# One program instead of two, four heads turned earlier, both mLSTM gates from one weight tile, and one activation table set asked for in two layer norms

## What is computed

```python
def third_block(x, ...):
    x = layer_norm(x, in_ln_g, in_ln_b)
    proj = x @ w_in[l]
    q, k, v, o_pre, i_pre, f_pre, z, xbc, dt_raw, g_a, g_b = jnp.split(proj, splits, -1)
    h_a = mlstm_branch(q, k, v, o_pre, i_pre, f_pre, ...)   # 8 heads; i_pre, f_pre: 8 columns each
    h_b = mamba2_branch(z, xbc, dt_raw, ...)
    merged = jax.nn.sigmoid(g_a) * (h_a @ p_a[l]) + jax.nn.sigmoid(g_b) * (h_b @ p_b[l])
    x = layer_norm(ALPHA * x + merged @ w_out[l], ln1_g[l], ln1_b[l])
    u = causal_dwconv(x @ w_up[l], f_conv_w[l], f_conv_b[l])
    u_gate, u_val = jnp.split(u, 2, -1)
    return layer_norm(ALPHA * x + (jax.nn.silu(u_gate) * u_val) @ w_down[l], ln2_g[l], ln2_b[l])
```

## Time and profile before

| | |
|---|---|
| median of 3 runs | 2726.02 us (2725.89 to 2728.17) |
| profiled execution, its own time | 2728.42 us |
| its span, first to last instruction | 2726.6 us |
| PE busy | 2544.7 us, 93% |
| PEld busy | 2024.6 us, 74% |
| DVE busy | 1384.9 us, 51% |
| ACT busy | 650.0 us, 24% |
| POOL busy | 1537.7 us, 56% |
| mean granted clock of PE | 0.965 |

### The profile page before, as it was taken

How to read it: one execution, slowest core, us unless ns; L and a number is a source line. 1 busy time by engine, 2 the same in 40 slices (tenths; PEclk the granted TensorE clock), 3 DMA queues, 4 the chain that set the end, 5 groups by cost and what they waited for, 6 DMA issues and landing times. The chain is left out here.

```text
span 2726.6 us, 32321 instructions
## 1 busy us (share of the span) xinstructions
PE 2544.7 (93%) x11714; PEld 2024.6 (74%) x11714; DVE 1384.9 (51%) x1929; ACT 650.0 (24%) x1047; POOL 1537.7 (56%) x1039
## 2 busy tenths in 40 slices
PE   6998999999989997799999998899998998999997
PEld 4885678888777773588967876766887886878775
DVE  6886651221489997668024335133356144535354
ACT  2116620110353344330022123123113222200002
POOL 2640266766688884468625745424762665566551
PEclk8999999999999998899999999899999999999998
DMA  8640023233222221122221322211331222223221
GB/s 268 218 158 1 31 78 93 93 94 107 93 78 78 77 92 46 50 93 93 77 77 47 108 63 66 68 53 47 108 93 32 77 79 91 77 93 93 93 71 42
DMA packets 231014, 231.36 MB, mean 85 GB/s; under 512 B 10011, under 2 KB 228860, under 8 KB 230780
## 3 DMA queue, kind: packets, MB, share of 16 engines
q1 hardware_dynamic: 228368, 228.87, 26.4%
q10 hardware_dynamic: 2540, 1.11, 0.2%
HBM read 227.86 MB, written 2.10 MB: 84 GB/s over the span
## 5 line engine op out<-in xcount | busy, mean ns | idle before, releaser
L1264 POOL TENSOR_TENSOR Wl<-raw,Wh 128x512 fp32r<-128x512 f32 (+4 forms) x772 | 1048.3, 1389 | 29.1 <-issue 7.6
L1258 POOL TENSOR_SCALAR Wh<-raw 128x2048 fp32r<-128x2048 f32 (+3 forms) x197 | 369.5, 1876 | 953.1 <-PE PS L1311 541.4
L1311 PE MATMUL PS<-Hh,Wh 128*128 128x512 f32 x1984 | 790.3, 398 | 76.4 <-POOL Wl L1264 24.8
L1311 PE MATMUL PS<-Hl,Wh 128*128 128x512 f32 x1984 | 783.3, 395 | 0.0
L1311 PE MATMUL PS<-Hh,Wl 128*128 128x512 f32 x1984 | 782.2, 394 | 0.0
L1311 PEld LDWEIGHTS PS<-Hh,Wh 128*128 128x128 f32 x1984 | 376.3, 190 | 176.5 <-issue 48.1
L1311 PEld LDWEIGHTS PS<-Hh,Wl 128*128 128x128 f32 x1984 | 376.3, 190 | 83.9 <-issue 1.5
L1311 PEld LDWEIGHTS PS<-Hl,Wh 128*128 128x128 f32 x1984 | 376.7, 190 | 80.0 <-issue 0.7
L1311 PE MATMUL PS<-Bh,Wh 128*128 128x512 f32 x688 | 271.5, 395 | 8.8 <-DVE Bl L2841 8.8
L1311 PE MATMUL PS<-Bl,Wh 128*128 128x512 f32 x688 | 270.0, 393 | 0.0
L1311 PE MATMUL PS<-Bh,Wl 128*128 128x512 f32 x688 | 269.8, 392 | 0.0
(11 more groups left out here) (442 smaller groups left out, 2885.1 us busy)
## 6 DMA issues: line engine op xcount, KB each, us to landing
raw<-in_w_in SPq DMA_DIRECT2D x44, 1024.0 KB, 5.8
raw<-in_w_ff SPq DMA_DIRECT2D x32, 1024.0 KB, 5.3
raw<-in_conv_w_in SPq DMA_DIRECT2D x24, 1024.0 KB, 5.1
raw<-in_ret_w_in SPq DMA_DIRECT2D x24, 1024.0 KB, 5.2
spare<-in_ada_w SPq DMA_DIRECT2D x20, 1024.0 KB, 7.2
raw<-in_w_up SPq DMA_DIRECT2D x20, 1024.0 KB, 5.4
raw<-in_w_out SPq DMA_DIRECT2D x8, 1024.0 KB, 5.0
raw<-in_conv_w_out SPq DMA_DIRECT2D x8, 1024.0 KB, 5.0
```

The lines of the kernel that those rows point to most:

```text
L1258: pool.tensor_scalar(st.Wh[0:rows, slot, k, 0:g.width], st.raw_slot(slot)[0:rows, k, 0:g.width], 1.0, 1.0, ALU.mult, ALU.mult)
L1264: ins = pool.tensor_tensor(st.Wl[0:rows, slot, k, 0:g.width], st.raw_slot(slot)[0:rows, k, 0:g.width], st.Wh[0:rows, slot, k, 0:g.width].b ...
L1311: mm = pe.matmul(out, lhs, rhs, start=(k == parts[0][0] and n == 0), stop=(k == parts[-1][0] and n == 2))
```

## The change

All of it is done at once:

- **One program.** Stages w1 and w2 become one: one list of steps, one weights_part with one set of semaphores (weights_sems). The semaphores that zeroing clears are given back there, so that later parts can have them.
- **One tile for both gates.** i_rows and f_rows become gate_rows, 40 columns wide: two loads (pieces) put the input gate's 8 columns at column 0 and the forget gate's at column 32 of the same slot; the columns between hold what was there and are multiplied too. ACT copies partitions 0 to 7 and 32 to 39 of the result to their two places (two_gates). All later tiles move to the other slot.
- **Four heads turned early.** The turns of heads 0 and 1 (PE) go between two pieces of ga in head 7, ahead of the values of head 6, those of heads 2 and 3 ahead of head 7's last scores; the first waits for all 32 exponentials. On ACT the four outs go around the squares of head 6, ahead of ga's last take.
- **One table set.** A CentredNorm without pre (l1 and l2) asks for the set that has both Exp and Ln at its start.

```diff
...
 M_HEADS, M_CONV = 8, 4
+GATE_ROWS = 32
 S_HEADS, S_GROUPS, S_CONV = 16, 4, 4
...
         CURRENT.remove(s)
+    for step in steps:
+        if isinstance(step, Part):
+            step.ctx.close()
     return part
...
         act.drain()
+        if not self.pre:
+            act.preload_act_table_set(EXP_AND_LOG)
         for c in range(KC if self.pre else 0):
...
-    def __init__(self, w, rhs, rounds, phases, stride=2 * TW, mode="features", row0=0, rows=D, width=TW, ready=None):
+    def __init__(self, w, rhs, rounds, phases, stride=2 * TW, mode="features", row0=0, rows=D, width=TW, ready=None, pieces=None):
         self.w, self.rhs, self.rounds, self.phases, self.mode = w, rhs, rounds, phases, mode
         self.row0, self.rows, self.stride, self.width, self.ready = row0, rows, stride, width, ready
-        self.k_order = None
+        self.k_order, self.pieces = None, pieces
         self.made_by = self.beside = self.beside_load = self.after = self.early = None
...
+
+    def loads(self):
+
+        return len(self.pieces) if self.pieces else 1 + (self.rows % P > 0)
...
-def weights_part(nc, st, name, steps):
+def weights_sems(nc, name):
     ctx = ExitStack()
-    landed = sems(nc, ctx, name, "landed0 landed1")
-    freed = sems(nc, ctx, name, "acc_free0 acc_free1")
-    split_done, multiplied, staged, posted, taken, asked, made, rounded = sems(
-        nc, ctx, name, "split_done multiplied staged posted taken asked made rounded")
+    return ctx, sems(nc, ctx, name, "landed0 landed1 acc_free0 acc_free1 split_done multiplied staged posted "
+                                    "taken asked made rounded")
+
+
+def weights_part(st, ctx, weight_sems, steps):
+
+    landed, freed = weight_sems[0:2], weight_sems[2:4]
+    split_done, multiplied, staged, posted, taken, asked, made, rounded = weight_sems[4:]
     base = stage0 = post = made0 = 0
...
         for j in range(g.rounds * len(g.phases)):
-            landings[(base + j) % 2] += 1 + (g.rows % P > 0)
+            landings[(base + j) % 2] += g.loads()
         base += g.rounds * len(g.phases)
...
-        per = 1 + (g.rows % P > 0)
+        per = g.loads()
         before = sum((g.base + q) % 2 == slot for q in range(p))
...
                 dst = st.raw_slot(slot)
+                if g.pieces:
+                    for at, c0, n in g.pieces:
+                        sp.dma_start(dst[:, 0:full, at:at + n], body[:, :, ds(c0, n)]).then_inc(landed[slot], 16)
+                    continue
                 sp.dma_start(dst[:, 0:full, 0:g.width], body[:, :, ds(c0, g.width)]).then_inc(landed[slot], 16)
...
             pe.wait_ge(scaled, h + 1)
+            if h == 0:
+                pe.wait_ge(exped, NB * M_HEADS)
             if h >= 2:
...
             beside.products(pe, j, (k0 + h % 2,))
+            if h == M_HEADS - 1:
+                turn(0)
+                turn(1)
             if h:
...
             beside.products(pe, j, (k0 + 3,))
+            if h == M_HEADS - 1:
+                turn(2)
+                turn(3)
             score(h, 3)
         values(M_HEADS - 1)
-        for h in range(GROUP):
-            turn(h)
         rows_beside.products(pe, 0, range(KC))
...
                 beside.take(act, h // 2 - 1)
+            if h == M_HEADS - 1:
+                out(0)
+                out(1)
             if h:
                 squares(h - 1)
+        out(2)
+        out(3)
         beside.take(act, M_HEADS // 2 - 1)
...
         rstd(1)
-        for h in range(GROUP):
-            out(h)
         rows_beside.take(act, 0)
...
-def program(nc, t, out, stop=None):
+def program(nc, t, out):
     ctx = ExitStack()
...
-        def rows_to(c, n):
-            def act(e, acc, i, p):
-                return e.activation(st.A[0:n, c, :], acc[0:n, 0, :], ACT.Copy)
-            return act
+        def two_gates(e, acc, i, p):
+            e.activation(st.A[0:M_HEADS, 24, :], acc[0:M_HEADS, 0, :], ACT.Copy)
+            return e.activation(st.A[0:M_HEADS, 25, :], acc[GATE_ROWS:GATE_ROWS + M_HEADS, 0, :], ACT.Copy)
...
                                   pre=(pcols("final_norm_2", 8), 1e-6))
-            i_rows, f_rows = (
-                tiles(w3, H, 1, at_i + n * M_HEADS, width=M_HEADS, act=rows_to(24 + n, M_HEADS), order="gate",
-                      ready=norm7_8.ready) for n in range(2))
-            gates, gates_rest = gates_parts(nc, st, f_rows.all_staged)
+            gate_rows = tiles(w3, H, 1, at_i, width=GATE_ROWS + M_HEADS, act=two_gates, order="gate",
+                              ready=norm7_8.ready, pieces=[(GATE_ROWS * n, at_i + n * M_HEADS, M_HEADS) for n in range(2)])
+            gates, gates_rest = gates_parts(nc, st, gate_rows.all_staged)
             return [
                 gate0, gate1, second, out0, out1, norm7_8.part,
-                i_rows, f_rows, gates,
+                gate_rows, gates,
                 conv_tiles(st, w3, H, 4, 0, 0, "mc", "m_conv_b_3", M_CONV),
...
+        weight_ctx, weight_sems = weights_sems(nc, "w")
         start, steps = first_steps()
...
         steps += more[:-1] + [zeroing([attention, *more[:-3]])] + more[-1:] + third_steps()
-        stage(nc, *start, weights_part(nc, st, "w1", steps))
-        if stop != "w1":
-            stage(nc, weights_part(nc, st, "w2", fourth_steps() + fifth_steps()))
+        steps += fourth_steps() + fifth_steps()
+        stage(nc, *start, weights_part(st, weight_ctx, weight_sems, steps))
```

## The result

The changed kernel takes **2703.84 us** (median of 4 runs, 2702.3 to 2710.42) against 2726.14 us for the kernel before (4 runs, 2725.89 to 2728.17): ratio 0.992, 95% interval 0.9904 to 0.9936, a gain of 22 us. Forecast were 2696 us and a gain of 30.3, with a range up to 2703. The sign was right, the size was not. The profiled execution took 2710.42 us of its own time, 2708.5 us of span; its places are compared with those of before's 2726.6 us.

The account below looks back on a forecast made before the run. PE, busy 93% of the span, was taken as the bound. Terms 7.9 - 0.2 + 14.2 + 5.8 + 2.6 = 30.3 us, taken from the median 2726.0 us, gave 2696 us, range 2690 to 2703.

Parts of the forecast that it names:

- What bounds the kernel: Whole kernel: PE is busy 93% of the span; only its idle time, lower clock or dropped work can be won.
- Heads turned early: End of the memory: turning heads 0 to 3 inside head 7 gains 5.8 us, bounds 4.1 and 6.7.
- n78: Mean subtraction beside POOL's early split of the conv weights: 0.2 us lost, bounds 0 and 1.1.
- Gates: Gate tiles and conv: one 40-column tile drops matmuls and a PE stop, gaining 7.9 us, bounds 5.9 and 9.0.
- rival (c): Turns and third conv tile: new short waits let the clock fall, 1.7 us each; 2699 us, chance 10%.
- Border: Between the two stages: early weight loads and split remove PE's stop and lower clock, gaining 14.2 us, lower bound 11.
- Rival (b): Border, head 0: ga's early split costs PE what it hides, 11 us gained for 14.2; 2699 us, chance 12%.
- Rival (e): Border: it is not what holds the first weights, and PE waits as before; 2710 us, chance 4%.
- Table set: Layer norms l1 and l2: no table load between Ln and Exp, gaining 2.6 us, bounds 0 and 2.6.
- Rival (d): Layer norms: a table load stays between Ln and Exp; 2698 us, chance 4%.
- Rival (f): Later stage's hardware loops on PE: shifted code stalls the issue, slower, 2738 us with seven stops; chance 2%.
- (a): Gates: DVE's chain does not bind, or less, 9.0 us gained for 7.9; 2694.6 us, chance 12%.

Follow-up runs that it names:

- e4: Kernel before with only the early turns of four heads moved in: 2726.36 us, ratio 1.0001.
- e2: Changed kernel with POOL's split of the second o tile held until DVE has scaled all eight heads: 2697.53 us, ratio 0.9882.
- e6: Changed kernel with two gate tiles, late turns and no table request, so only the border is changed against before: 2713.67 us, ratio 0.9949.
- e1: The changed kernel run again with no edit: 2707.46 us, ratio 0.9927 to the kernel before.
- e9: Changed kernel with POOL's split of the second o tile held behind the scaling, run again on another chip: 2697.4 us, ratio 0.9888.
- e3: Changed kernel with the turns of heads 0 to 3 put back behind the last values: 2708.25 us, ratio 0.9926.
- e12: Kernel before with only the one gate tile of 40 columns, run again for a profile: 2722.68 us, ratio 0.9986.
- e7: Kernel before with only the table set asked for in the two layer norms: 2720.67 us, ratio 0.9976.
- e11: Kernel before with only the table set request, run again: 2722.32 us, ratio 0.9983.

## Why the prediction was wrong

**What bounds the kernel** was right: every gain and loss found in a profile is idle time, lower clock or dropped matmuls of PE.

**Heads turned early is the step that failed.** It was to give 5.8 us and gave 0 (e4, ratio 0.9992 to 1.001, so within 3 us). The sentence "four heads take 3.2 us" took DVE's duration from a stretch in which POOL was idle and moved it into one in which POOL is not. The same paragraph moved dt's tile ahead by 7 us, and did not follow what its end releases: POOL's next split. It even kept "DVE's chain 0.9 us shorter with POOL idle" as a bound, so POOL's place was thought of, with the wrong sign. With the split held, the step measures 6.2 us in place against before and the forecast of 5.8 stands: mechanism and sizes were right but for that neighbour. From the start of keeping head 7 to the last scaling it forecast 7.9 us (1860.9 to 1868.8); it is 7.3 us in e2 (1838.60 to 1845.92) and 13.4 us in the changed kernel (1843.64 to 1856.99).

The rule of the Trainium skill (SBUF — State Buffer, Who interferes with whom) was in the prediction, but as one for two SBUF inputs only. It was applied at n78, and the same collision was priced at head 0's cuts. There it cost nothing: the subtraction took 5.43 us instead of 4.90, yet from DVE's last takes of out1 to the first gate product it is 22.07 us, before 22.03; the cuts are hidden. The scaling has one tensor input and was not checked against it; the runs show that it is held as well.

**Gates: a term of the sum was mis-sized**, 7.7 forecast, 5.5 measured. 5.4 us of matmuls and the stop of 1.95 us went as expected. The new stop is 1.8 us, not 1.2, because the chain took 13.5 us, not 12.7, with POOL's split now running beside all of its end; with that "short enough to keep the clock" was no longer about a stop of 1.2 us, and 1.7 us were lost again in four profiles of six. The result lies below the lower bound of 5.9 us, which had the chain 0.3 us slower and not 0.8. That was rival (c) at this one place.

**Border** was right: 14.2 forecast, 14.6 in e6; the changed kernel's own profile has 11.4 because its clock fell there. Rival (b) fell: the cuts beside the early split take longer, but PE doesn't stand for them. Rival (e) fell.

**Table set** was right in place, 2 x 1.28 us. Rival (d) fell. **Rival (f)** fell: PE's stops without a releaser are the same two, 7.8 us in all.

**The sum, corrected**: 5.5 + 14.6 + 0 + 2.6 = 22.7 us, or 20.3 with the 2.4 us that the o tiles lose behind the early turns. Measured were 22.3 us by the medians of the result and 19.9 by the ratio of e1. Had POOL's split stayed behind the scaling, the forecast would have held: e2 and e9, at 2697.5 and 2697.4 us, are 1.5 us off it. Part of that is luck: their places add up to 5.5 + 14.6 + 6.2 + 2.6 = 28.9 us, with the gates short by 2.2 us, and 29.5 to 32.2 us were measured (medians and ratios); the rest, like that of the table set, has no place. None of the rivals named this case; (b) had the same collision, but at the border, and (a) let DVE's chain be early, not late. The range was cut at 2703 by rivals of 3 us each, while a stretch with three engines meeting at new times can lose all it gains.

## What to carry to other kernels

When a step lets PE finish a tile earlier, follow the slot that the tile frees to POOL's next split, and see what DVE does at that moment. A duration read where the neighbour was idle is not a duration for where it isn't; price it again from a row with both busy. And a gain that consists of the clock kept is only one if the new stop is clearly shorter than the one that lost it.

## What the runs showed of the hardware

- DVE's scaling of a 128x128 float32 block from and to SBUF, with one tensor input, takes 0.28 us alone, 1.99 us beside a POOL instruction of 2.05 us and 1.35 us beside POOL instructions of 1.31 us. POOL's long one was lengthened in two of three profiles (2.05 and 2.04 us, 1.90 in e1); beside the gates' chain POOL's four short ones took 6.39 us instead of 5. One DVE instruction gets in for each of POOL's short ones, so short DVE instructions beside long POOL ones fare worst: sixteen of them went from 3.23 to 9.26 us.
- PE's clock falls behind stops of 1.8 us in some executions and not in others of the same kernel: 1.81 us with a fall in the changed kernel, 1.77 us without one in its second profile and in e9. Length alone doesn't decide: 1.79 us with a fall in e2, e3 and e12, 1.86 us with one in e4, but 1.87 and 1.88 us without in e7, e11 and e6. Matmuls of 512 columns then start 0.43 us apart instead of 0.23.
- A border between two programs costs this kernel 14.6 us, 12.2 us of it a stop of PE while the first weight tile is loaded and split.
